# Page keys and probabilities turned by VectorE, scores in array quarters, the last tile's rows over all sample stages

## The reference

```python
ckv_all = jnp.concatenate([cache_ckv[l][page_table].reshape(DB, past_len, KV_LORA), ckv], axis=1)
kr_all = jnp.concatenate([cache_krope[l][page_table].reshape(DB, past_len, QK_ROPE), krope], axis=1)
...
s = (jnp.einsum('bqhc,bkc->bhqk', q_abs, ckv) + jnp.einsum('bqhr,bkr->bhqk', q_pe, krope)) * scale
p = jax.nn.softmax(s, axis=-1)
o_lat = jnp.einsum('bhqk,bkc->bqhc', p, ckv)
...
act = jax.nn.gelu(jnp.einsum('thkd,td->thk', expert_u[eid], tb))     # eid: 128 experts a token
return jnp.einsum('thk,thkd->td', g * act, expert_v[eid])
```

## Time and profile before

| what | us |
|---|---|
| median of 3 runs | 4627.76 |
| lowest, highest | 4603.08, 4628.37 |
| the profiled execution | 4633.7 |
| its span, first to last instruction | 4631.9 |
| PE, DVE, ACT, POOL busy | 3421.8, 2701.1, 735.0, 2585.1 |
| mean DMA rate over the span | 334 GB/s |
| mean granted TensorE clock, share of full | 0.889 |

### The profile page before, as it was taken

How to read it: one execution, slowest core, us unless ns; L and a number is a source line. 1 busy time by engine, 2 the same in 40 slices (tenths; PEclk the granted TensorE clock), 3 DMA queues, 4 the chain that set the end, 5 groups by cost and what they waited for, 6 DMA issues and landing times.

```text
span 4631.9 us, 38219 instructions
## 1 busy us (share of the span) xinstructions
PE 3421.8 (74%) x10984; PEld 1623.3 (35%) x10984; DVE 2701.1 (58%) x6250; ACT 735.0 (16%) x2170; POOL 2585.1 (56%) x2069
## 2 busy tenths in 40 slices
PE   6877777777777777777787778777877766777882
PEld 3333333433333333323342334233433323444430
DVE  1156568645865576656765686458655775544305
ACT  1112010211021112101120103111211101222210
POOL 0006666666666666676566666666666644665201
PEclk9888988999989898999889889989898987888996
DMA  5659999999989998999899998999899998999762
GB/s 166 204 201 343 402 371 347 332 402 398 357 308 395 400 379 313 360 402 374 333 349 402 381 352 326 402 399 362 303 384 395 369 327 304 312 317 331 256 227 73
DMA packets 606531, 1546.72 MB, mean 334 GB/s; under 512 B 92114, under 2 KB 149083, under 8 KB 606323
## 3 DMA queue, kind: packets, MB, share of 16 engines
q0 software_dynamic: 297216, 1082.26, 62.0%
q1 hardware_dynamic: 308084, 458.32, 28.0%
q10 hardware_dynamic: 1024, 3.70, 0.2%
HBM read 1533.93 MB, written 10.13 MB: 333 GB/s over the span
## 4 chain that ended last, share of the span: by engine, by line
DMA 34%; PE 28%; DVE 16%; POOL 10%; issue 8%; ACT 2%; SPq 1%; another core or an unknown queue 0%; POOLq 0%; DVEq 0%; ACTq 0%
DMA rows<-in_peer_v_dram,pe_id 22%; POOL rows L595 10%; PE PS L655 10%; PE PS L995 9%; DMA rows<-in_peer_u_dram,pe_id 4%; DVE rows L1639 3%; DMA wbuf<-in_peer_w_q_dram 2%; DMA wbuf<-in_w_oa_dram 2%; PE PS L640 1%; DMA wbuf<-in_w_ob_dram 1%; DVE xr L1664 1%; DMA wbuf<-in_w_in_dram 1%; PE PS L765 1%; PE PS L746 1%; PE PS L954 1%
## 5 line engine op out<-in xcount | busy, mean ns | idle before, releaser
L595 POOL DMA_INDIRECT rows<-in_peer_u_dram,pe_id x1024 | 1290.2, 1260 | 1065.2 <-DVE dots L1639 457.4
L995 PE MATMUL PS<-rows,diags 128*128 128x512 f32 x2356 | 1319.7, 692 | 638.2 <-DMA rows<-in_peer_v_dram,pe_id 489.2
L595 POOL DMA_INDIRECT rows<-in_peer_v_dram,pe_id x1024 | 1275.5, 1246 | 721.2 <-PE PS L995 445.8
L1639 DVE CUSTOM_DVE_ANT_0 rows<-rows,px 128x1024 f32<-128x1024 f32 x1024 | 1246.3, 1224 | 735.9 <-DMA rows<-in_peer_u_dram,pe_id 710.8
L655 PE MATMUL PS<-wbuf,xt 128*128 128x512 f32 (+1 forms) x2304 | 1051.5, 599 | 54.7 <-DMA wbuf<-in_w_in_dram 37.6
L995 PEld LDWEIGHTS PS<-rows,diags 128*128 128x128 f32 x2356 | 457.6, 211 | 1299.7 <-issue 1011.0
L655 PEld LDWEIGHTS PS<-wbuf,xt 128*128 128x128 f32 x2304 | 450.5, 202 | 657.3 <-issue 505.1
L1664 DVE SCALAR_TENSOR_TENSOR xr<-rows,gcoef,xr 128x1024 f32<-128x1024 f32 x435 | 558.0, 1283 | 173.7 <-issue 170.5
L655 PE MATMUL PS<-wbuf,wide 128*128 128x512 f32 (+1 forms) x828 | 392.6, 615 | 59.7 <-ACT wide L1060 16.0
L655 PEld LDWEIGHTS PS<-wbuf,wide 128*128 128x128 f32 x828 | 162.6, 202 | 276.6 <-issue 179.9
L1757 ACT ACTIVATE diags<-ident,gcoef 128x128 f32<-128x128 f32 x589 | 210.2, 398 | 75.7 <-DVE gcoef L1655 75.7
(11 more groups left out here) (302 smaller groups left out, 2489.9 us busy)
## 6 DMA issues: line engine op xcount, KB each, us to landing
wbuf<-in_w_in_dram SPq DMA_DIRECT2D x396, 512.0 KB
wbuf<-in_peer_w_q_dram SPq DMA_DIRECT2D x144, 512.0 KB
wbuf<-in_w_ob_dram SPq DMA_DIRECT2D x72, 512.0 KB
wbuf<-in_w_out_dram SPq DMA_DIRECT2D x72, 512.0 KB
KV<-in_cache_ckv_dram SPq DMA_DIRECT2D x176, 128.0 KB
wbuf<-in_w_oa_dram SPq DMA_DIRECT2D x36, 512.0 KB
rows<-in_peer_u_dram,pe_id POOLq DMA_INDIRECT x1028, 5.2
rows<-in_peer_v_dram,pe_id POOLq DMA_INDIRECT x1024
```

What stands on the lines that cost most here:

```text
L595: pool.indirect_dma_start(row_slot(kind, n), None, a["peer_u" if kind == "u" else "peer_v"][0], bass.IndirectOffsetOnAxis(ap=pe_id[t % 2][ ...
L995: last = nc.tensor.matmul(bank[3 + 4 * c], diag(n), row_slot("v", n)[:, c * 512:(c + 1) * 512], start=start, stop=stop)
L1639: V.tensor_tensor_reduce(out=row, in0=row, in1=px[:, :], scale=1.0, scalar=0.0, op0=ALU.mult, op1=ALU.add, accum_out=dots[:, at_:at_ + 1]) ...
```

## The change

The nine PE transposes of a chunk and their ACT copies go. DVE turns the chunk in 32x32 blocks, with one transpose of 128x1024 and one of 128x128 (`turn`, now in `dve_sample`), straight into one of two buffers `turned`. In such a block layout 32 channels of 32 tokens lie together, so the scores are made in quarters of the array: nine products over 32 rows each (eight blocks of key channels, one of rotary channels), for four quarters of tokens, each with 32 rows, 32 columns and 32 partitions of output (`score`). The queries are laid out for that by 16 small ACT copies into `qrep` and, per request, one copy into one of two `qsc`. The probabilities are turned by DVE as well (`weights`), in one transpose.

The softmax of request b-1 is now spread over the chunks of request b, and scores alternate between two bank sets (`scores_at`). The number of page slots stays at 12, and the values still free them. SAMPLE_ROW_YIELDS goes from 80 to 128, so the 74 pairs lie over all places of the sample's front.

```diff
-        qr4 = cut(NH * NB)
+        qrep = qb[:, 0:9 * NH * NB]
+        qr4 = qrep[:, 8 * NH * NB:9 * NH * NB]
...
-        qsc = cut(2 * 32)
-        qsr = cut(P)
+        qsc = [decay_t[:, 0:9 * 32], q_decay[:, 0:9 * 32]]
...
+        turned = [KV[:, VAT + PAGE_SLOTS * P + i * 1152:VAT + PAGE_SLOTS * P + (i + 1) * 1152] for i in range(2)]
+
+        def scores_at(b):
+            return 4 * 512 if b % 2 == 0 else 0
...
+            def score(b, c):
+                s_turned.wait(pe, b, c + 1)
+                if c == 0:
+                    s_staged.wait(pe, b)
+                    s_exp.wait(pe, b - 2)
+                blocks_of = turned[c % 2][:, 0:4 * KVL].rearrange("p (j k m) -> p k j m", j=4, m=32)
+                at_ = scores_at(b) + c * P
+                for k in range(9):
+                    for q in range(4):
+                        quarter = slice(32 * q, 32 * (q + 1))
+                        last = nc.tensor.matmul(
+                            PS[quarter, at_:at_ + P], qsc[b % 2][quarter, k * 32:(k + 1) * 32],
+                            blocks_of[quarter, k] if k < 8 else turned[c % 2][quarter, 4 * KVL:4 * KVL + P],
+                            start=(k == 0), stop=(k == 8))
+                last.then_inc(s_sc_filled.sem, 1)
...
-                for c in range(NCH):
-                    if 1 < c + 1 < NCH:
-                        turn(b, c + 1)
-                    score(c)
-                    if c < NCH - 2:
-                        yield "page"
...
+            def maxima(b):
...
+            def values(b):
                 s_weight.wait(pe, b)
+                s_pt.wait(pe, b)
...
+            pe.wait_ge(s_setup, 1)
             for b in range(NB):
-                yield from attend(b)
+                for c in range(NCH):
+                    if c == NCH - 2:
+                        new_key(b)
+                    score(b, c)
+                    if b > 0 and c < 5:
+                        (maxima, max_column, totals, values, outputs)[c](b - 1)
+                    yield "page"
+            for stage in (maxima, max_column, totals, values, outputs):
+                stage(NB - 1)
...
+            for q in range(4):
+                for i in range(4):
+                    last = nc.scalar.activation(
+                        qrep[32 * q:32 * (q + 1), 0:8 * NH * NB].rearrange("p (c k n) -> p c k n", c=2, k=4)[:, :, i],
+                        AS.bank(0, "qabs")[32 * i:32 * (i + 1), 0:2 * NH * NB].rearrange("p (c n) -> p c n", c=2), ACT.Copy)
+            last.then_inc(AS.drained, 1)
...
+            stage_queries(0)
             for b in range(NB):
-                yield from attend(b)
+                for c in range(NCH):
+                    if b > 0 and c in (1, 3, 4):
+                        {1: exponents, 3: scaled, 4: turned_out}[c](b - 1)
+                    if c == NCH - 1 and b + 1 < NB:
+                        stage_queries(b + 1)
+                    yield "page"
+            for stage in (exponents, scaled, turned_out):
+                stage(NB - 1)
...
+            def turn(g):
+                if g >= NB * NCH:
+                    return
+                dve.wait_ge(s_pages[g % PAGE_SLOTS], 8 * 16 * (g // PAGE_SLOTS + 1))
+                s_sc_filled.wait(dve, 0, g - 1)
+                V.transpose(turned[g % 2][:, 0:4 * KVL], page_at(g))
+                V.transpose(turned[g % 2][:, 4 * KVL:4 * KVL + P], krope_at(g)).then_inc(s_turned.sem, 1)
...
+            def weights(b):
+                s_exp.wait(dve, b, 1)
+                s_pv.wait(dve, b - 1)
+                V.transpose(WK[:, D:2 * D], WK[:, 0:D]).then_inc(s_pt.sem, 1)
...
+            turn(0)
+            turn(1)
             for b in range(NB):
-                yield from one(b)
+                for c in range(NCH):
+                    if b > 0 and c < 3:
+                        (maxima, row_maxima, weights)[c](b - 1)
+                    if c == 4:
+                        half_max(b, 0)
+                    if c == NCH - 1:
+                        s_new_filled.wait(dve, b)
+                        s_diff.wait(dve, b - 1)
+                        link.mark(V.tensor_copy(snew[:, 0:NH], bank[6][0:1, 420:420 + NH]))
+                    turn(b * NCH + c + 2)
+                    yield "page"
+            for stage in (maxima, row_maxima, weights):
+                stage(NB - 1)
...
-SAMPLE_ROW_YIELDS = 80
+SAMPLE_ROW_YIELDS = 128
```

More of the change, by code:

```diff
@@ L881, in pe_sample_attention, with new_key @@
         def pe_sample_attention(pe):
[L883 to L898 removed]
+            def score(b, c):
[13 more added lines that the diff above has]
+                last.then_inc(s_sc_filled.sem, 1)
+            def new_key(b):
                 s_ota.wait(pe, b - 1)
@@ L907, in attend @@
                 last.then_inc(s_new_filled.sem, 1)
-                def score(c):
-                    s_kt_drained.wait(pe, b, 3 * c + 3)
-                    if c == 0:
-                        s_staged.wait(pe, b)
-                        s_pt_drained.wait(pe, b - 1)
-                    for part in range(3):
-                        for j in range(4):
-                            last = nc.tensor.matmul(
-                                PS[32 * j:32 * (j + 1), 4 * 512 + c * P:4 * 512 + (c + 1) * P],
-                                qsc[:, part * 32:(part + 1) * 32] if part < 2 else qsr[:, 32 * j:32 * (j + 1)],
-                                ktb[c % 2][:, part * 512 + j * P:part * 512 + (j + 1) * P] if part < 2 else ktb[c % 2][:, 1024:1024 + P],
-                                start=(part == 0), stop=(part == 2))
-                    last.then_inc(s_sc_filled.sem, 1)
@@ L934, in attend, with totals @@
                 s_rowm.wait(pe, b)
                 nc.tensor.matmul(bank[6][:, 384:385], rowm4, ident[0:1, 0:1], start=True, stop=True).then_inc(s_mcol.sem, 1)
-                yield "page"
+            def totals(b):
                 s_exp.wait(pe, b)
-                for i in range(NCH):
-                    last = nc.tensor.transpose(bank[4 + i // 4][:, i % 4 * P:(i % 4 + 1) * P], WK[:, i * P:(i + 1) * P], ident[:, :])
-                    if i % 4 == 3:
-                        last.then_inc(s_pt_filled.sem, 1)
@@ L1266, in attend, with scaled @@
                                      scale=SCALE).then_inc(s_exp.sem, 1)
-                if b + 1 < NB:
-                    keys(b + 1, 0)
-                yield "page"
-                for i in range(2):
-                    s_pt_filled.wait(act, b, i + 1)
-                    s_pv.wait(act, b - 1)
-                    nc.scalar.activation(WK[:, D + i * 512:D + (i + 1) * 512], bank[4 + i], ACT.Copy).then_inc(s_pt_drained.sem, 1)
-                if b + 1 < NB:
-                    keys(b + 1, 1)
+            def scaled(b):
                 s_pv_new.wait(act, b)
```

100 lines of the change are left out of this document (27 added, 73 removed).

## The result

The changed kernel takes 4734.1 us (median of 4 runs, 4725.8 to 4749.4), the kernel before 4628.1 beside it: ratio 1.0244, interval 1.0204 to 1.0284. It is slower by 106 us. The forecast was 4649, and the range ended at 4715, so the prediction was wrong. The profiled execution of the changed kernel spans 4735.4 us, that of the kernel before 4631.9.

A forecast was written before the change was run, and what follows sets the result against it. Attention was taken as near its DMA limit, with SyncE's page issue nearly as full. Front -16, attention -28, weight stage +43 and choice of experts +22 gave +21 us on 4627.8: 4649 us, range 4550 to 4715.

The forecast's parts named there:

- The mechanism that it called decisive: Attention: SyncE must issue all eight page groups between two value stages, in series with the rest; 59.8 us a loop.
- The choice of experts: Stage before the sample's own experts: ten v, tile 7's final norm and a wait on DVE, +22 us.
- the rest of the loop: Attention: the part of each loop beside SyncE's eight groups, put at 9.4 us, 2.4 of it for rows.
- The first eleven places: Start of attention, pages in hand: 4.6 us a place by PE's work without values, 51 us.
- The last request's end: End of attention: four groups, landing, turn and score 31 us, then the last request's unhidden chain 16.6 us.
- Front: Front and retention: 19 fewer gathers gain 13 us, the moved norm 6.4, new copies cost 3; together -16 us.
- Weight stage: Sample's weight blocks: 18.5 pairs of rows come in, 144.5 us becomes 188, +43.
- The rival with 65.4 us a loop: Attention: SyncE stays as slow as now, 7.0 us a group; total +58, 4686 us; chance 0.25.
- the other three stages: Front and retention -16, weight stage +43, choice of experts +22 us; +49 together.
- My own 59.8: Attention: forecast loop between two value stages, 9.4 us plus 8 groups at 6.3 us.
- My -28: Whole attention stage: forecast 458 us against 486.4.
- the last rival: Attention: score quarters run one after another, 10.3 us a page, stage 841 us, total about +390, 5020; chance 0.09.

## Why the prediction was wrong

*Right.* The mechanism that it called decisive is there: 15.6 us of wait for values in each of SyncE's loops, VectorE's 169.5 us for pages, 6.2 us a group against 6.3 taken. Two more slots or earlier keys remove most of it, and alone it makes a loop of 53.0 us. The transpose took 1.24 us (taken: 1.2) and is off the path. The choice of experts came at +21 (taken: +22). Undisturbed, at the full clock, a group's scores took 2.17 us (taken: 2.6), so the quarters run side by side and that rival is out. The Trainium skill's rule on it ("TensorEngine Tiling (Array Packing)", Restrictions and Gotchas) does not hold here: four row tiles, each writing 32 partitions of its own, wrote one bank at 30 ns a record.

*The term that failed: the rest of the loop,* "9.4 us plus 8 groups". Without rows it measured 5.7, and the forecast's own parts without its 2.4 for a pair add up to 7.0, so the parts that were listed are sound. With rows it was 15.6. I priced the rows as 2.4 us of VectorE. That was too little, and it left out TensorE. Pairs delay the turn of the eighth group (4.3 of the 9.9 us that the rows add to the rest) and what follows it (5.7), where TensorE does pairs at half clock (3.78 us) and VectorE waits for its totals. With the pairs moved ahead of the turn the ratio did not change. With fewer score instructions the kernel gained 36 us in all and the rest of a loop was 13.3. How much of the rest is the pairs' own work, and how much late pages, late instructions and clock, was not split further. Six loops: +32 us.

*The first eleven places,* taken at 4.6 us "by PE's work without values", 51 us, measured 72.5: +21. The price of 2.6 us for a group's scores came from an undisturbed burst of the old kernel. Here the twelve bursts took 3.7 us on average (in the loops 3.4), which is 13 us. TensorE also waits 6.6 us for tile 6's norm, which I moved here as if VectorE's room were all that counted. Both terms are estimates from the trace and not tested apart: with 20 of 36 score matmuls the stretch took 50.5 us, but with all 36 and the pairs moved it took 51.3, both on other chips. The last request's end was 54.8 us for the 47.6 taken: +7.

*Front.* I gave it 13 of the 28 us that 19 gathers fewer take, and 6.4 for the norm; all of it came to 5. The step that put the gain at half of the DMA work had no row behind it.

*Weight stage.* 18.5 pairs came in at 351 GB/s and not at tile 7's 395; the straight line between 0 and 32 pairs, 211, and my 188 had the 199 in their middle.

*The chances.* The rival with 65.4 us a loop had the right size for a wrong reason: it needed 7.0 us a group, and the groups took 6.2. The forecast and it shared one assumption, a rest of 9.4, and the range took no uncertainty from it although it stands in series six times. The sum of the other three stages was also low (+70 for the +49 taken). And the test that I did not make: at equal dealing, what would the old attention do? SyncE at 6.3 would have given it 50.4 us, measured 51.9. My own 59.8 for the new one was already slower. Seen like that, the attention stage holds two changes with opposite signs: counted from the first score, the dealing takes 67 us off it and the new order puts 104 on. My -28 was their sum and looked harmless. In the last rival, 841 for 486 with +49 elsewhere is +404 and not +390; nothing hangs on it.

## What to carry over

When buffers are freed at a later point of the loop, count the issues between two frees and everything in series with them, on every engine of the chain, each at the price it has beside the real traffic; then vary that term in the range as often as it repeats. If a change has two parts, forecast each alone against the same base: a gain from one can hide a loss in the other. And issue ahead whatever becomes free early (here keys, free after the transpose) before waiting for what becomes free late.

## What was not expected of the hardware

Small instructions can come late. Of the 144 weight loads and matmuls of a group's scores, the loads waited 51.2 us for "issue" in 385 us of the changed kernel, and 0.9 in 259 without rows. In such a stretch SyncE took 4.8 us from the last issue of one group to the first of the next (4119.47 to 4124.28), against 1.9 in the quiet. Gathers alone do not set the amount: the run with the pairs moved had as many of them (DMA share 0.70, 0.71 in the changed kernel), on another chip, and from 3917 to 4298:

```profile
PEld PS L898 <- issue: 17.6, 15, 1.5
```

Its bursts took 2.6 us on average, those of the changed kernel 3.4. What makes the instructions late, no run here shows.

SyncE took 5.9 us for eight page DMAs with their numbers in the quiet, and 5.9 to 7.0 beside the gathers. ScalarE issued eight key DMAs in 5.4 us. As an issuer it made the old kernel 1.3 to 1.5% slower; in the changed one the loop grew by 3.7 us, and the total did not move beyond its interval.

VectorE turned 128x1024 of f32 in 32x32 blocks in 1.24 us and 128x128 in 0.27. The Trainium skill ("VectorE: DVE Perf Modes", Rules for kernel authors) says that for a transpose of 32x32 within a bank VectorE's is the fastest. No run here turns such blocks another way. What the trace shows is the price behind it: 36 score matmuls a group of pages where 12 and nine transposes had been, bursts of 3.4 us on average in the loops of the changed kernel, against 1.2 and 1.5 in the kernel before at 128 places.
